# Twenty-four expert tiles' scores in plain float32, computed in the routing and table stages, in a transformer kernel with a product-key expert layer

## The chip, the cores and the metric

One Trainium2 chip, of which the kernel uses one core. The metric is the device time of one execution of the whole program in microseconds (us). Engines are named as in the profile: PE is TensorE (PEld its weight loads), DVE VectorE, ACT ScalarE, POOL GpSimd, SP SyncE, which here only issues DMAs.

## The reference, cut to what matters

A first block works on 512 tokens of width 1024 (a two-way gated recurrence, a convolution of 31 taps, attention, a merge, and an expert layer); a second block of two further layers follows. The change touches the convolution's place in time and the expert layer, which has 128 x 128 = 16384 experts:

```
def _peer(h, wq, k1, k2, u_tab, v_tab):
    def block(t):
        q = (t @ wq).reshape(PEER_BLOCK, PEER_HEADS, 2, PEER_DQ // 2)
        s1 = jnp.einsum('thd,nd->thn', q[:, :, 0], k1).astype(jnp.float32)
        s2 = jnp.einsum('thd,nd->thn', q[:, :, 1], k2).astype(jnp.float32)
        ...
        expert = (jnp.take_along_axis(i1, ci // PEER_TOPK, axis=-1) * PEER_NKEYS
                  + jnp.take_along_axis(i2, ci % PEER_TOPK, axis=-1))
        g = jax.nn.softmax(score, axis=-1).astype(t.dtype)
        act = jax.nn.gelu(jnp.einsum('thkd,td->thk', u_tab[expert], t))
        return jnp.einsum('thk,thkd->td', g * act, v_tab[expert]).astype(t.dtype)
```

## The kernel before, in words

The kernel is a row of phases with a barrier of all engines between them. Four of them matter here.

**Mixers** (`phase_mixers`). After eight recurrence heads come four rounds `attend(i)` of attention. In a round, DVE normalises and rotates the rows, and then goes through 8 units: the peak of the next unit's scores (L1476), a reciprocal (L1483), some convolution taps (`taps(count)`, L1435: one 128x512 multiply-add each, 248 in all, taken in order from a single list), and the rest part of a weight tile. ACT forms the softmax of a unit after its peak (L1206), normalises it (L1222), and copies out weight products; PE fills weight products between the transposes (L998). The hand-written order puts 8 taps ahead of the wait for `a_rstd` in rounds 1 to 3, 3 taps behind it, 10 taps in unit 0 and 7 in each other unit. When the list is used up, `taps` does nothing.

**Routing** (`phase_routing`). For each of 8 heads PE multiplies two query tiles (L1787, plain float32, 512 columns, 8 matmuls per half) and the key scores (L1795); ACT copies them out (L1818, L1823) and does the exponential of the head before (L1810); DVE finds the top 16 (from L1895 on), and POOL and DVE look up the indices.

**Table** (`phase_expert_table`). The choices of 384 of the 512 tokens are turned into a dense table of gate weights, 4 tokens a group, 96 groups. Per group DVE builds two one-hot tiles (L2000, L2004, rings of 4), PE multiplies them (L2016, four plain float32 matmuls of 128 columns), ACT copies the result out (L2027), and SP stores 4 MB to DRAM after each 16 groups (L2036).

**Experts** (`phase_experts`). The 384 tokens go through all 16384 experts densely: 128 tiles of 128 experts, 2 a step, 64 steps. Each tile has a score product (24 matmuls of 384 columns, L2205 to L2207: the operands are cut into an upper and a rest part of type float32r, and three of the four cross products are taken), a gelu (L2280), a multiplication with the table's rows (L2340), a cut of that product (L2285, L2325), and an output product into six PSUM banks (18 matmuls of 512 columns, L2221 to L2225). Both the tile of `peer_u` and that of `peer_v` (512 KB each) are cut by ACT (L2264, L2272) and DVE (L2325). PE's order in step s is: scores of step s+1, outputs of step s. The other 128 tokens' chosen rows are gathered by POOL with indirect DMAs (L2176, L2184), four of 512 KB a step, and handled by DVE (`dots`, L2351; `own_add`, L2367). DVE's order in step s: `cut_u(s+2)`, `cut_v(s+1)`, `dots(s+1)`, `weights(s)`, `weigh(s+1)`, two `own_add`. ACT's: `cut_u(s+2)`, `cut_v(s+1)`, `own_gelus(s)`, `gelus(s+1)`. ACT's `cut_v(s+1)` waits for the outputs of step s-1. Steps 0, 1, 62 and 63 are written out; the 60 between them are a loop with two steps in its body.

## Time and the profile before

| | us |
|---|---|
| median of 3 executions | 4812.54 (4811.25 to 4816.73) |
| the profiled execution | 4815.9 |
| its span in the profile | 4814.1 |
| attention rounds of the mixers | about 696 to 1085 |
| routing | about 1469 to 1677 |
| table | about 1678 to 1850 |
| experts | about 1850 to 2926 |

Over the span PE is busy 90%, DVE 55%, ACT 38%, POOL 11%. The profile is read by stage: a window of it gives each engine's busy time there, the granted clock of PE as a share of full speed, and the share of the 16 DMA engines' time that is used. Matmuls are pipelined, so that the time between two starts, not the duration of one, is what a matmul costs.

### The profile page before, as it was taken

How to read it: one execution, taken by the hardware profiler on the slowest of the kernel's cores; microseconds unless marked ns; L12 is line 12 of the kernel's file. 1: busy time of each engine (PE TensorE's matmuls, PEld its weight loads, DVE VectorE, ACT ScalarE, POOL GpSimd, SP SyncE). 2: the span in 40 equal slices, each digit the busy share in tenths (PEclk: the TensorE clock that was granted, in tenths of full speed). 3: DMA queues.
4: the chain of work that ended last, by engine and by line, in shares of the span. 5: the costliest groups of instructions: out<-in, count | busy, mean ns of one | idle time of the engine just before them, and what ended most of it. 6: DMA issues, size and time to landing. Idle time of an engine off the chain costs nothing. (4 is left out here: it accounts for less than half of the span.)

```text
span 4814.1 us, 56280 instructions
## 1 busy us (share of the span) xinstructions
PE 4348.4 (90%) x20979; PEld 3540.2 (74%) x20979; DVE 2663.7 (55%) x4645; ACT 1814.3 (38%) x2539; POOL 526.0 (11%) x308
## 2 busy tenths in 40 slices
PE   8988888879998367999999997999999999999998
PEld 6866765646874256999999995777878877777887
DVE  0777758773437897767677675334343333434332
ACT  1665654443421033333333333345232233643322
POOL 0000000000003502334333430000000000000000
PEclk9999999989999699999999998999999999999999
DMA  7111101103322037887787771211323322122332
GB/s 263 58 40 44 40 31 49 43 1 108 92 63 67 5 140 281 281 279 270 282 278 276 274 273 65 70 53 59 99 88 97 96 84 70 51 77 84 102 97 81
DMA packets 196090, 579.09 MB, mean 120 GB/s; under 512 B 17345, under 2 KB 66753, under 8 KB 194369
## 3 DMA queue, kind: packets, MB, share of 16 engines
q1 hardware_dynamic: 158032, 435.34, 27.4%
q0 software_dynamic: 36864, 134.23, 7.9%
q10 hardware_dynamic: 1008, 7.03, 0.4%
q8 instruction: 119, 1.95, 0.2%
q14 instruction: 67, 0.54, 0.0%
HBM read 549.27 MB, written 27.26 MB: 120 GB/s over the span
## 5 line engine op out<-in xcount | busy, mean ns | idle before, releaser
L402 DVE TENSOR_TENSOR tile_rest<-tile_raw,tile_up 128x1024 fp32r<-128x1024 f32 (+2 forms) x288 | 338.7, 1181 | 786.4 <-ACT tile_up L393 786.2
L410 PE MATMUL layer_psum<-hn_up,tile_up 128*128 128x512 f32 x1344 | 534.7, 398 | 21.5 <-DVE hn_rest L497 21.5
L411 PE MATMUL layer_psum<-hn_up,tile_rest 128*128 128x512 f32 x1344 | 527.7, 393 | 0.0
L412 PE MATMUL layer_psum<-hn_rest,tile_up 128*128 128x512 f32 x1344 | 527.3, 392 | 0.0
L393 ACT ACTIVATE tile_up<-tile_raw 128x1024 fp32r<-128x1024 f32 (+2 forms) x288 | 291.4, 1018 | 370.3 <-PE layer_psum L412 368.5
L2205 PE MATMUL ex_psum<-ex_t_up,ex_u_up 128*128 128x384 f32 x1024 | 344.5, 336 | 9.1 <-ACT ex_prod L2280 4.9
L2207 PE MATMUL ex_psum<-ex_t_rest,ex_u_up 128*128 128x384 f32 x1024 | 344.4, 336 | 0.0
L2206 PE MATMUL ex_psum<-ex_t_up,ex_u_rest 128*128 128x384 f32 x1024 | 343.9, 336 | 0.0
L410 PEld LDWEIGHTS layer_psum<-hn_up,tile_up 128*128 128x128 f32 x1344 | 255.7, 190 | 82.4 <-issue 30.0
L2225 PE MATMUL ex_psum<-ex_v_up,ex_prod_rest 128*128 128x512 f32 x768 | 300.0, 391 | 0.0
L2223 PE MATMUL ex_psum<-ex_v_rest,ex_prod_up 128*128 128x512 f32 x768 | 299.9, 390 | 0.0
L2221 PE MATMUL ex_psum<-ex_v_up,ex_prod_up 128*128 128x512 f32 x768 | 298.7, 389 | 0.0
L411 PEld LDWEIGHTS layer_psum<-hn_up,tile_rest 128*128 128x128 f32 x1344 | 255.6, 190 | 54.4 <-issue 1.9
L412 PEld LDWEIGHTS layer_psum<-hn_rest,tile_up 128*128 128x128 f32 x1344 | 255.1, 190 | 53.9
L2272 ACT ACTIVATE ex_v_up<-tT 128x1024 fp32r<-128x1024 f32 x128 | 128.8, 1052 | 290.3 <-PE ex_psum L2225 286.2
L2325 DVE TENSOR_TENSOR ex_v_rest<-tT,ex_v_up 128x1024 fp32r<-128x1024 f32 x128 | 151.2, 1222 | 143.9 <-ACT ex_v_up L2272 143.8
L601 PE MATMUL mx_psum<-x_up,mx_w_up 128*128 128x512 f32 x480 | 200.3, 417 | 9.4 <-DVE mx_w_rest L563 9.4
L2205 PEld LDWEIGHTS ex_psum<-ex_t_up,ex_u_up 128*128 128x128 f32 x1024 | 193.5, 189 | 12.5 <-issue 10.1
L1842 POOL TENSOR_TENSOR rt_hot<-rt_place,consts 128x1024 f32<-128x1024 f32 x16 | 30.8, 1928 | 1556.4 <-DVE rt_place L1952 1505.4
L2206 PEld LDWEIGHTS ex_psum<-ex_t_up,ex_u_rest 128*128 128x128 f32 x1024 | 193.4, 189 | 2.4
L2207 PEld LDWEIGHTS ex_psum<-ex_t_rest,ex_u_up 128*128 128x128 f32 x1024 | 193.2, 189 | 0.0
L602 PE MATMUL mx_psum<-x_up,mx_w_rest 128*128 128x512 f32 x480 | 190.9, 398 | 0.0
(450 smaller groups left out, 9981.3 us busy)
## 6 DMA issues: line engine op xcount, KB each, us to landing
ex_u<-in_peer_u SPq DMA_DIRECT2D x128, 512.0 KB, 4.3
tT<-in_peer_v SPq DMA_DIRECT2D x128, 512.0 KB
tile_raw<-in_w_gu SPq DMA_DIRECT2D x88, 512.0 KB, 3.6
xT<-in_w_head SPq DMA_DIRECT2D x56, 512.0 KB, 3.6
mod_w<-in_w_ada SPq DMA_DIRECT2D x48, 512.0 KB, 4.7
mg_w_raw<-in_w_merge SPq DMA_DIRECT2D x48, 512.0 KB
expert_table<-et_rows SPq DMA_DIRECT2D x6, 4096.0 KB
ex_rows<-expert_table SPq DMA_DIRECT2D x64, 384.0 KB, 6.2
```

The lines of the kernel that those rows point to most:

```text
L393: self.nc.scalar.activation(self.up[:, n % self.SLOTS, 0:blocks, :], self.raw[n % self.RAWS][:, 0:blocks, :], ACT.Copy).then_inc(self.up_r ...
L402: self.nc.vector.tensor_tensor(out=self.rest[:, n % self.SLOTS, 0:blocks, :], in0=self.raw[n % self.RAWS][:, 0:blocks, :], in1=self.up[:, ...
L410: self.nc.tensor.matmul(dst, w_up, up, start=first, stop=False)
L411: self.nc.tensor.matmul(dst, w_rest, up, start=False, stop=False)
L412: return self.nc.tensor.matmul(dst, w_up, rest, start=False, stop=last)
L601: self.nc.tensor.matmul(dst, w_up, up[:, d, :], start=d == 0, stop=False)
L2205: nc.tensor.matmul(dst, u_up[par, t][:, d, :], t_up[:, d, :], start=d == 0, stop=False)
L2206: nc.tensor.matmul(dst, u_rest[par, t][:, d, :], t_up[:, d, :], start=False, stop=False)
L2207: last = nc.tensor.matmul(dst, u_up[par, t][:, d, :], t_rest[:, d, :], start=False, stop=d == DB - 1)
L2221: nc.tensor.matmul(dst, prod_up[par, t][:, cols], v_up[par, t][:, rows, :], start=first, stop=False)
L2223: nc.tensor.matmul(dst, prod_up[par, t][:, cols], v_rest[par, t][:, rows, :], start=False, stop=False)
L2225: last = nc.tensor.matmul(dst, prod_rest[par, t][:, cols], v_up[par, t][:, rows, :], start=False, stop=final)
```

## The change

Three things are altered.

1. Of the 128 expert tiles, 24 (`EARLY`: tiles 2, 8, 13, 18, 24 and so on to 125, never two in a step) get their scores before the experts phase. A class `EarlyScores` loads such a tile of `peer_u`, multiplies it uncut with the tokens in plain float32 (8 matmuls of 384 columns in place of 24), applies gelu, and stores 128x384 numbers to DRAM. Twelve tiles are handled in routing (one each behind the key scores of heads 1 to 6, six behind those of head 7), and twelve in the table phase (one matmul ahead of each group's four).
2. In the experts phase those 24 tiles have no load or cut of `peer_u`, no score product and no gelu; their stored scores (192 KB) are loaded and DVE weighs them in place. The other 104 run through rings counted by their own number q. The loop over the steps is written out in full; so is SP's loop in routing.
3. The taps of the convolution are dealt anew: 14 in place of 8 ahead of the wait for `a_rstd` in rounds 1 to 3, 4 in place of 10 in unit 0 of all rounds.

```diff
+EARLY = [(2 * k + 1) * NKEYS // 48 for k in range(24)]
+EARLY_ROUTING = 12
...
                 if i > 0:
-                    taps(8)
+                    taps(14)
...
                         rests_behind(plan.chain[i][:2])
-                        taps(10)
+                        taps(4)
...
+class EarlyScores:
+    SLOTS = 3
+    def __init__(self, ph, io, mem, banks, first, count):
+        self.io, self.mem, self.banks, self.first, self.count = io, mem, banks, first, count
+        self.u = [ph.sb(f"early_u{n}", [P, DB, P]) for n in range(self.SLOTS)]
+        self.out = [ph.sb(f"early_out{n}", [P, T_DENSE]) for n in range(2)]
+        self.landed = [ph.sem(f"early_landed{n}") for n in range(self.SLOTS)]
+        self.stored = [ph.sem(f"early_stored{n}") for n in range(2)]
+        self.scored, self.gelu_ready = ph.sem("early_scored"), ph.sem("early_gelu_ready")
+    def load(self, sp, e):
+        if e >= self.count:
+            return
+        if e >= self.SLOTS:
+            sp.wait_ge(self.scored, START + e - self.SLOTS + 1)
+        sp.dma_start(self.u[e % self.SLOTS][:],
+                     self.io["peer_u"][EARLY[self.first + e]]).then_inc(self.landed[e % self.SLOTS], 16)
+    def store(self, sp, e):
+        sp.wait_ge(self.gelu_ready, START + e + 1)
+        sp.dma_start(self.mem.early[self.first + e], self.out[e % 2][:]).then_inc(self.stored[e % 2], 16)
+    def all_stored(self, sp):
+        for half in range(2):
+            sp.wait_ge(self.stored[half], START + 16 * len(range(half, self.count, 2)))
+    def block(self, nc, pe, e, d):
+        if d == 0:
+            pe.wait_ge(self.landed[e % self.SLOTS], START + 16 * (e // self.SLOTS) + 16)
+            if e >= 2:
+                pe.wait_ge(self.gelu_ready, START + e - 1)
+        ins = nc.tensor.matmul(self.banks[e % 2][:, 0:T_DENSE], self.u[e % self.SLOTS][:, d, :],
+                               self.mem.tT[:, d, 0:T_DENSE], start=d == 0, stop=d == DB - 1)
+        if d == DB - 1:
+            ins.then_inc(self.scored, 1)
+    def gelu(self, nc, act, e):
+        act.wait_ge(self.scored, START + e + 1)
+        if e >= 2:
+            act.wait_ge(self.stored[e % 2], START + 16 * (e // 2))
+        nc.scalar.activation(self.out[e % 2][:], self.banks[e % 2][:, 0:T_DENSE],
+                             ACT.Gelu_apprx_tanh).then_inc(self.gelu_ready, 1)
...
+        early = EarlyScores(ph, io, mem, (B[7], B[6]), 0, EARLY_ROUTING)
         block = ph.block(w)
+        def early_of(h):
+            return range(0) if h == 0 else range(h - 1, h if h < HEADS - 1 else EARLY_ROUTING)
         @block.sync
         def _(sp):
             sp.dma_start(keys[:], io["peer_k"]).then_inc(keys_loaded, 16)
-            with sp.Fori(0, HEADS // 2) as i:
-                for t in range(4):
+            for h in range(HEADS):
+                i, hh = h // 2, h % 2
+                for half in range(2):
+                    t = 2 * hh + half
                     load_tile(sp, w, 0, t, i, io["w_peer_q"][i * 2 + t // 2, t % 2])
+                if h == 1:
+                    for e in range(early.SLOTS):
+                        early.load(sp, e)
+                if h > 2:
+                    for e in early_of(h - 2):
+                        early.store(sp, e)
+                        early.load(sp, e + early.SLOTS)
+            for h in range(HEADS - 2, HEADS):
+                for e in early_of(h):
+                    early.store(sp, e)
+                    early.load(sp, e + early.SLOTS)
+            early.all_stored(sp)
...
+                for e in early_of(h):
+                    for d in range(DB):
+                        early.block(nc, pe, e, d)
...
+            pe.wait_ge(early.gelu_ready, START + EARLY_ROUTING)
...
+                for e in early_of(h):
+                    early.gelu(nc, act, e)
...
+        early = EarlyScores(ph, io, mem, (B[7], B[6]), EARLY_ROUTING, len(EARLY) - EARLY_ROUTING)
...
             for n in range(GROUPS):
+                early.block(nc, pe, n // DB, n % DB)
...
+                if n % DB == DB - 1:
+                    early.gelu(nc, act, n // DB)
         @block.sync
         def _(sp):
-            for turn in range(GROUPS // SUBS):
-                sp.wait_ge(unpacked, START + (turn + 1) * SUBS)
-                dst = mem.table[turn:turn + 1, :, :, :].rearrange("o p j t -> p (o j) t")
-                sp.dma_start(dst, rows[turn % 2][:]).then_inc(stored[turn % 2], 16)
+            for e in range(early.SLOTS):
+                early.load(sp, e)
+            for e in range(early.count):
+                if (e + 1) * DB % SUBS == 0:
+                    turn = (e + 1) * DB // SUBS - 1
+                    sp.wait_ge(unpacked, START + (turn + 1) * SUBS)
+                    dst = mem.table[turn:turn + 1, :, :, :].rearrange("o p j t -> p (o j) t")
+                    sp.dma_start(dst, rows[turn % 2][:]).then_inc(stored[turn % 2], 16)
+                early.store(sp, e)
+                early.load(sp, e + early.SLOTS)
+            early.all_stored(sp)
...
+        late = {j: q for q, j in enumerate(j for j in range(NKEYS) if j not in EARLY)}
+        soon = {j: k for k, j in enumerate(EARLY)}
+        def late_of(s):
+            return [late[j] for j in range(s * G, s * G + G) if j in late]
...
-        u_up, u_rest = ring("u_up", [P, DB, P], F32R), ring("u_rest", [P, DB, P], F32R)
+        u_up, u_rest = ([sb(f"{name}{n}", [P, DB, P], F32R) for n in range(4)] for name in ("u_up", "u_rest"))
+        early = [sb(f"early{n}", [P, N]) for n in range(2)]
...
+        def whole(j):
+            return early[soon[j] % 2][:] if j in soon else prod[:, j % G, :]
...
-            for s in range(2):
-                step(s, s % 2, s)
-            with eng.Fori(1, STEPS // 2 - 1) as i:
-                for par in range(2):
-                    step(i * 2 + par, par, None)
-            for s in range(STEPS - 2, STEPS):
+            for s in range(STEPS):
...
             def load_u(s, n):
-                for t in range(G):
-                    if begun(n, 1):
-                        sp.wait_ge(u_cut, START + (s - 1) * G + t + 1)
-                    sp.dma_start(u[t], io["peer_u"][s * G + t]).then_inc(u_landed[t], 16)
+                for j in range(s * G, s * G + G):
+                    if j in late:
+                        q = late[j]
+                        if q >= G:
+                            sp.wait_ge(u_cut, START + q - G + 1)
+                        sp.dma_start(u[q % G], io["peer_u"][j]).then_inc(u_landed[q % G], 16)
+                    else:
+                        k = soon[j]
+                        if k >= 2:
+                            sp.wait_ge(prod_cut, START + EARLY[k - 2] + 1)
...
             def scores(s, par, n):
-                for t in range(G):
-                    pe.wait_ge(u_cut, START + s * G + t + 1)
-                    if begun(n, 1):
-                        pe.wait_ge(gelu_ready, START + (s - 1) * G + t + 1)
-                    dst = B[t][:, 0:N]
+                for q in late_of(s):
+                    pe.wait_ge(u_cut, START + q + 1)
+                    if q >= 2:
+                        pe.wait_ge(gelu_ready, START + q - 1)
+                    dst = B[q % 2][:, 0:N]
+                    up, rest = u_up[q % 4], u_rest[q % 4]
                     for d in range(DB):
-                        nc.tensor.matmul(dst, u_up[par, t][:, d, :], t_up[:, d, :], start=d == 0, stop=False)
-                        nc.tensor.matmul(dst, u_rest[par, t][:, d, :], t_up[:, d, :], start=False, stop=False)
-                        last = nc.tensor.matmul(dst, u_up[par, t][:, d, :], t_rest[:, d, :], start=False,
-                                                stop=d == DB - 1)
+                        nc.tensor.matmul(dst, up[:, d, :], t_up[:, d, :], start=d == 0, stop=False)
+                        nc.tensor.matmul(dst, rest[:, d, :], t_up[:, d, :], start=False, stop=False)
+                        last = nc.tensor.matmul(dst, up[:, d, :], t_rest[:, d, :], start=False, stop=d == DB - 1)
                     last.then_inc(scored, 1)
...
             def cut_u(s, par, n):
-                for t in range(G):
-                    act.wait_ge(u_landed[t], START + s * 16 + 16)
-                    if begun(n):
-                        act.wait_ge(scored, START + (s - 1) * G)
-                    nc.scalar.activation(u_up[par, t][:], u[t], ACT.Copy).then_inc(u_up_ready, 1)
+                for q in late_of(s):
+                    act.wait_ge(u_landed[q % G], START + q // G * 16 + 16)
+                    if q >= 4:
+                        act.wait_ge(scored, START + q - 3)
+                    nc.scalar.activation(u_up[q % 4][:], u[q % G], ACT.Copy).then_inc(u_up_ready, 1)
...
             def gelus(s, par, n):
                 for t in range(G):
-                    act.wait_ge(scored, START + s * G + t + 1)
-                    if begun(n, 1):
-                        act.wait_ge(prod_cut, START + (s - 1) * G + t + 1)
-                    nc.scalar.activation(prod[:, t, :], B[t][:, 0:N], ACT.Gelu_apprx_tanh).then_inc(gelu_ready, 1)
-                    act.wait_ge(weighed, START + s * G + t + 1)
+                    j = s * G + t
+                    if j in late:
+                        q = late[j]
+                        act.wait_ge(scored, START + q + 1)
+                        if begun(n, 1):
+                            act.wait_ge(prod_cut, START + j - G + 1)
+                        nc.scalar.activation(whole(j), B[q % 2][:, 0:N], ACT.Gelu_apprx_tanh).then_inc(gelu_ready, 1)
+                    act.wait_ge(weighed, START + j + 1)
                     if begun(n):
                         act.wait_ge(step_filled, START + s - 1)
-                    nc.scalar.activation(prod_up[par, t][:], prod[:, t, :], ACT.Copy).then_inc(prod_up_ready, 1)
+                    nc.scalar.activation(prod_up[par, t][:], whole(j), ACT.Copy).then_inc(prod_up_ready, 1)
...
+                for q in late_of(s):
+                    cut(u_up_ready, u_cut, q + 1, u_up[q % 4][:], u[q % G], u_rest[q % 4][:])
...
             def weigh(s, par, n):
                 for t in range(G):
-                    dve.wait_ge(gelu_ready, START + s * G + t + 1)
+                    j = s * G + t
+                    if j in late:
+                        dve.wait_ge(gelu_ready, START + late[j] + 1)
+                    else:
+                        dve.wait_ge(early_landed[soon[j] % 2], START + soon[j] // 2 * 16 + 16)
                     dve.wait_ge(rows_landed[par], START + (s - par) * 8 + 16)
-                    part = prod[:, t, :].rearrange("p (b k) -> p b k", k=BLOCK)
+                    part = whole(j).rearrange("p (b k) -> p b k", k=BLOCK)
                     nc.vector.tensor_tensor(out=part, in0=part, in1=rows[par][:, :, t * BLOCK:(t + 1) * BLOCK],
                                             op=ALU.mult).then_inc(weighed, 1)
-                    cut(prod_up_ready, prod_cut, s * G + t + 1, prod_up[par, t][:], prod[:, t, :],
-                        prod_rest[par, t][:])
+                    cut(prod_up_ready, prod_cut, j + 1, prod_up[par, t][:], whole(j), prod_rest[par, t][:])
...
+            mem.early = nc.dram_tensor("early_scores", (len(EARLY), P, T_DENSE), F32, kind="Internal").ap()
```

## Rows read from the trace of the kernel before

**Rows 1.** windows: us, busy time by engine (count), PE clock, DMA share, GB/s

```profile
1875.00:1925.00 50.00, 49.00 (x239) 44.69 (x240) 39.19 (x51) 22.67 (x34) 20.23 (x13) 0.97 0.96 349
2100.00:2300.00 200.00, 200.00 (x1016) 182.42 (x1015) 140.90 (x182) 73.17 (x109) 78.44 (x49) 1.00 0.80 276
3500.00:4500.00 1000.00, 956.49 (x4379) 773.52 (x4378) 390.65 (x450) 367.23 (x434) 0.00 (x0) 0.98 0.27 82
```

**Rows 2.** timeline of PE in the experts: start us, duration us, line

```profile
2299.82 0.39 PE L2223 MATMUL ex_psum<-ex_v_rest,ex_prod_up 128*128 128x512 f32 x1
...
2303.45 0.39 PE L2225 MATMUL ex_psum<-ex_v_up,ex_prod_rest 128*128 128x512 f32 x1
2303.68 0.33 PE L2205 MATMUL ex_psum<-ex_t_up,ex_u_up 128*128 128x384 f32 x1
...
2309.94 0.33 PE L2205 MATMUL ex_psum<-ex_t_up,ex_u_up 128*128 128x384 f32 x1
...
2320.22 0.33 PE L2205 MATMUL ex_psum<-ex_t_up,ex_u_up 128*128 128x384 f32 x1
```

**Rows 3.** DVE in the same step; in brackets the idle time before

```profile
2305.03 2.36 DVE L2325 TENSOR_TENSOR ex_v_rest<-tT,ex_v_up 128x1024 fp32r<-128x1024 f32 x2 [2.27 <-ACT ex_v_up L2272]
2307.31 1.22 DVE L2351 CUSTOM_DVE_ANT_0 ex_more<-ex_more,ex_own_t 128x1024 f32<-128x1024 f32 x1
...
2314.37 2.60 DVE L2367 SCALAR_TENSOR_TENSOR ex_own_out<-tT,ex_weight,ex_own_out 128x1024 f32<-128x1024 f32 x2
2316.89 2.35 DVE L2325 TENSOR_TENSOR ex_u_rest<-ex_u,ex_u_up 128x1024 fp32r<-128x1024 f32 x2
```

**Rows 4.** DMA traffic of the experts, 2100 to 2900

```profile
DMA packets 92582, 218.96 MB, mean 274 GB/s; under 512 B 6879, under 2 KB 43743, under 8 KB 92580
...
q8 instruction: 1, 0.02, 0.0%
...
ex_u<-in_peer_u SPq DMA_DIRECT2D x94, 512.0 KB, 4.2
```

**Rows 5.** DMA traffic of the experts, 1875 to 1925

```profile
DMA packets 7503, 17.46 MB, mean 349 GB/s; under 512 B 561, under 2 KB 3633, under 8 KB 7499
```

**Rows 6.** DMA queues of a later stage, 3500 to 4500

```profile
q8 instruction: 35, 0.57, 0.2%
```

**Rows 7.** timeline of PE in routing

```profile
1503.10 13.90 PE L1787 MATMUL rt_psum<-tT,rt_w 128*128 128x512 f32 x32
1516.83 2.01 PE L1795 MATMUL rt_psum<-rt_keys,rt_qT 128*128 128x128 f32 x16
1518.68 13.90 PE L1787 MATMUL rt_psum<-tT,rt_w 128*128 128x512 f32 x32
```

**Rows 8.** timeline of ACT in routing, third head

```profile
1518.88 0.60 ACT L1823 ACTIVATE rt_s<-rt_psum 128x512 f32<-128x512 f32 x1 [0.36 <-PE rt_psum L1795]
```

**Rows 9.** timeline of DVE in routing, third head

```profile
1525.93 1.63 DVE L1895 MAX8 rt_val<-rt_s 128x8 f32<-128x128 f32 x8
```

**Rows 10.** timeline of PE at the end of routing

```profile
1673.91 2.15 PE L1802 MATMUL rt_psum<-consts,rt_found 128*128 128x128 f32 x9 [59.07 <-DVE rt_found L1885]
```

**Rows 11.** timeline of the table stage

```profile
1701.12 1.13 PE L2016 MATMUL et_psum<-et_second,et_first 128*128 128x128 f32 x8 [0.50 <-DVE et_second L2004]
...
1702.52 0.69 DVE L2000 TENSOR_TENSOR et_first<-consts,i1T 128x512 f32<-128x512 f32 x1
...
1702.75 1.13 PE L2016 MATMUL et_psum<-et_second,et_first 128*128 128x128 f32 x8 [0.50 <-DVE et_second L2004]
```

**Rows 12.** timeline of DVE in attention rounds 2 and 3

```profile
923.28 2.21 DVE L1454 SCALAR_TENSOR_TENSOR xT<-xT,params,at_work 128x1024 f32<-128x1024 f32 x2 [5.35 <-ACT at_work L1198]
...
943.50 7.83 DVE L1435 SCALAR_TENSOR_TENSOR convT<-at_upad,params,convT 128x512 f32<-128x512 f32 x10
...
1020.32 2.22 DVE L1454 SCALAR_TENSOR_TENSOR at_qk<-at_qk,params,at_work 128x1024 f32<-128x1024 f32 x2 [9.56 <-ACT at_work L1198]
```

**Rows 13.** timeline of PE in attention round 0, second unit

```profile
743.16 1.51 PE L998 MATMUL mx_psum<-consts,at_probs 128*128 128x128 f32 x6 [4.65 <-ACT at_probs L1222]
```

More of the change, by code:

```diff
@@ L1989, in phase_expert_table @@
         stored = [sem("stored0"), sem("stored1")]
+        early = EarlyScores(ph, io, mem, (B[7], B[6]), EARLY_ROUTING, len(EARLY) - EARLY_ROUTING)
+        assert early.count * DB == GROUPS
         block = ph.block()
@@ L2083, in phase_experts @@
         u_landed = [sem(f"u_landed{t}") for t in range(G)]
+        early_landed = [sem(f"early_landed{n}") for n in range(2)]
         v_landed = [sem(f"v_landed{t}") for t in range(G)]
@@ L2131, in load_u @@
             def load_u(s, n):
-                for t in range(G):
-                    if begun(n, 1):
-                        sp.wait_ge(u_cut, START + (s - 1) * G + t + 1)
-                    sp.dma_start(u[t], io["peer_u"][s * G + t]).then_inc(u_landed[t], 16)
+                for j in range(s * G, s * G + G):
[8 more added lines that the diff above has]
+                            sp.wait_ge(prod_cut, START + EARLY[k - 2] + 1)
+                        sp.dma_start(early[k % 2][:], mem.early[k]).then_inc(early_landed[k % 2], 16)
             def load_v(s, par, n):
@@ L2327, in cut_u @@
             def cut_u(s, par, n):
-                for t in range(G):
-                    cut(u_up_ready, u_cut, s * G + t + 1, u_up[par, t][:], u[t], u_rest[par, t][:])
+                for q in late_of(s):
+                    cut(u_up_ready, u_cut, q + 1, u_up[q % 4][:], u[q % G], u_rest[q % 4][:])
             def cut_v(s, par, n):
```

## The prediction

> **What bounds the kernel now.** I read the windows by stage first, then the timeline of PE inside a stage, then what DVE, ACT and the DMA queues do beside it. In the experts PE is the bound: in a window of 200 us it is busy for all 200, at full clock, while DVE is busy for 141, ACT for 73, and the DMA engines have a share of 0.80 [rows 1]. The reader is to see in the timeline that matmuls follow each other without a gap: 16 gaps between output matmuls take 3.63 us, 0.227 each, and 36 gaps between score matmuls 6.26 us, 0.174 each [rows 2]. A step is 2320.22 - 2303.68 = 16.54 us, which is 48 x 0.174 + 36 x 0.227 = 16.52. In the table stage it is DVE: it begins a group every 1.63 us and PE waits 0.50 us for it in each [rows 11]. In the last part of routing it is DVE with POOL: PE stands still for 59 us before the last transposes [rows 10]. In the attention rounds DVE, ACT and PE take turns, and PE waits 4.65 us in the second unit, behind DVE's ten taps [rows 12, 13].
>
> **Part 1, the score products taken out of the experts.** Each early tile removes 24 matmuls of 0.174 us, 4.18 us; 24 tiles make 100.2 us, all of it on the engine that sets the end. I take 100, if nothing else becomes the bound in the 24 shortened steps, which take 16.54 - 4.18 = 12.36 us.
>
> DVE: from its cut of v to the end of its cut of u it takes 2305.03 to 2319.24, 14.2 us with its waits [rows 3]. That is over 12.36, so in a shortened step DVE falls behind by up to 1.9 us, and gets back 2.3 in a full one; two shortened steps never follow each other, and a tile without a cut saves it half of 2.35 us once. What it falls behind with is the cut of v and the product of step s+1, which PE wants only after the scores of step s+2, some 12.4 + 8.3 us after the step's start. No wait of PE, cost 0. ACT is busy 37% and follows DVE.
>
> DMA: a step moves four loads and four gathers of 512 KB and 384 KB of rows, 4.59 MB, which at 16.54 us is 277 GB/s, as the traffic view has it (274) [rows 4]. A shortened step moves 4.26 MB (192 KB of stored scores in place of 512) in 12.36 us, 345 GB/s; the mean over the stage becomes (64 x 4.59 - 24 x 0.33) / 959 us = 298 GB/s. The highest rate shown is 349 GB/s, at a share of 0.96, in a stretch in which PE was busy 49 of 50 us [rows 1, 5]. Loads land in 4.2 us [rows 4] and are issued most of a step ahead. I take 0. The other end: if a shortened step moved only 274 GB/s it would take 15.5 us, 3.2 more, 76 us in all.
>
> The start of the stage loses a little: the second step's scores are shorter, and then PE waits for the first product. I take +1 (0 to +2).
>
> **Part 2, the loop written out.** PE is busy 200 of 200 us across some 12 step pairs and their branches, so there is nothing to win. The loop stays on the chip: one instruction packet in 800 us on queue q8 [rows 4]. Straight code fetches: 35 packets in 1000 us in a later stage [rows 6], in which PE issued 4379 matmuls and as many weight loads [rows 1], 250 instructions of PE a packet. The 64 steps hold 40 x 84 + 24 x 60 = 4800 matmuls and as many loads, some 39 packets, one per 25 us. The later stage takes them without PE stopping for long (956 us busy of 1000), though at a DMA share of 0.27; the 50 us of rows 5 hold written-out steps at 0.96. I take 0. The Trainium skill (Runtime: NRT & Kernel Launch, Instruction fetch mechanics) has the sequencer prefetch sequential code and warns of taken branches, not of straight code. By it the sum would be the same or better; the trace shows no cost of the branch.
>
> **Part 3, the same products in plain float32 in routing.** 16 matmuls of 512 columns take 1516.83 - 1503.10 = 13.73 us, 0.858 each [rows 7]; 384 columns are three quarters of that, 0.644, a tile 5.15 us. No row shows 384 columns, so the ends are 0.644 and 0.858. The third head's scores were copied out by 1519.5 [rows 8]; with one tile ahead of them it is 1524.6, and DVE takes them at 1525.93 [rows 9]: 1.3 us to spare. From there PE needs 15.6 (1518.68 - 1503.10) + 5.15 = 20.7 us a head, while DVE needs (1673.91 - 1525.93) / 6 = 24.7. PE's last six tiles end near 1523.8 + 5.15 + 4 x 20.7 + 15.6 + 30.9 = 1658, 16 us before the transposes that wait for DVE [rows 10]. SP, now with stores and loads between its weight tiles, waits for gelus that are done before the next tile's slot is free. ACT must change its function table twice a head, behind the copies that PE waits for. I take +1 (0 to +5, the third head at 0.858).
>
> **Part 4, the products in the table stage.** Per group PE has 8 records, half of 1518.68 - 1516.83 = 1.85 us, 0.925 [rows 7], plus 0.644, 1.57 us, against DVE's 1.63 [rows 11]. It fits by 0.06. The upper end, 0.858, gives 1.78 and 96 x 0.15 = +15 us. The stage also starts with a load of 4.2 us that PE must await, where it began 2 us behind DVE, and at a lower clock after that pause; DVE is held back by the ring of 4 once. I take +4 (0 to +15). The Trainium skill (FP8 and Floating Point Precision, TensorE Precision Notes) says true float32 takes 4 passes through the array: 4 x 0.174 = 0.70 as an estimate by that page, 1.62 us a group, still 0.01 under DVE; by it the sum stays and the margin is gone.
>
> At the end the store of the last scores stands behind a 4 MB store in SP's queue: +1 (0 to +2), with the phases' extra semaphores.
>
> **Part 5, the taps.** Ten taps take 7.83 us [rows 12], six 4.7. Taken out of unit 0 they let DVE give the next peak up to 4.7 us earlier, and PE's pause of 4.65 us there [rows 13] goes; all four rounds have one. Limits: the weight tile cut behind the taps must have been cut by ACT (half a us), so 4.2 a round, 17 in all (8 if units 1 to 7 are paced by PE's own work, 21 if the clock stays up too). The six taps set before `a_rstd` lie in idle time: 5.35 us in round 2 and 9.56 in round 3 [rows 12], against 4.7. If a round were without that idle, they would cost 4.7 there. The last round's extra taps fall where DVE waited for PE.
>
> **Sum** against the profiled execution (4815.9, span 4814.1): -100 + 1 + 0 + 1 + 4 + 1 - 17 = -110, so 4706. The median of the runs shown is 3.4 lower, so 4703.
>
> **Rivals.**
> *A, transfers set the shortened steps.* For it: 345 GB/s is close to the highest seen. Against: buffers reach over two steps, and the mean is only 298. At a rate halfway between 274 and 349, 312 GB/s, a shortened step takes 13.65 us, 1.3 more, 31 in all: 4734. It decides from where PE waits for a cut of u.
> *B, PE becomes the bound of the table stage.* 1.57 against 1.63 says little either way. With 0.1 us per group for the change between widths, 1.67 x 96 gives +4 beyond the stage's start, with 0.858 +11 beyond my +4: 4707 to 4714.
> *C, instruction fetch stops PE in the written-out experts (the other side).* 39 packets on engines that are 0.86 to 1 busy. If each were waited for as long as a load takes to land, 4.2 us, that is 164 us: 4867, slower. It turns to slower from 2.8 us a packet. Against it: straight steps ran at 49 of 50 us with the DMA engines at 0.96 [rows 1].
> *D, the taps bring nothing*, since PE paces the rounds anyway: 4720. Against it: PE's 4.65 us pause.
>
> **How the numbers follow.** My forecast 0.68, A 0.12, B 0.11, C 0.03, D 0.06. The forecast's own range is 4692 to 4715; A and D stretch the range to 4734, and the low end is taps at -21, table at 0 and the rest at their best. So 4690 to 4734, with about 0.15 left out. What this kernel's measurement can tell from no change is about 0.2%, 10 us; only C and a wide form of A come there or beyond: faster 0.96, same 0.01, slower 0.03.
>
> **What would show it.** In the profile after: score matmuls L2205's successors 832 each in place of 1024; PE busy near 100% in the experts and the stage some 99 us shorter; a shortened step of 12.4 us; the DMA share near 0.86; routing as long as before with PE busy to about 1658 on the old time axis; the table stage's idle time of PE per group fallen from 0.50 us to nearly none, and the distance of DVE's groups still 1.63; PE's pause of 4.65 us in the rounds gone. Wrong I would be if PE has idle time in the experts before a cut of u or by "issue", or if DVE waits for PE in each group of the table.

## The result and the profile after

The changed kernel takes 4688.7 us (median of 4 runs, 4684.14 to 4694.84) against 4814.64 (4 runs on the same chip, 4811.25 to 4816.99): ratio 0.974, 95% interval 0.9723 to 0.9757. It is 126 us faster. The forecast was 4703, with 4690 as the low end, so the time lies 1.3 us below the range.

The profiled execution took 4694.84 us, with a span of 4693.0, 121.1 less than before. Busy time over the whole span, and the instruction queue, from the profile page of the changed kernel:

```profile
PE 4343.6 (93%) x20787; PEld 3492.2 (74%) x20787; DVE 2632.9 (56%) x4621; ACT 1806.3 (38%) x2529; POOL 502.2 (11%) x308
q8 instruction: 156, 2.56, 0.2%
```

Windows of the changed kernel by stage (columns as in [rows 1]): the experts, the table stage, routing, the four attention rounds.

```profile
1875.00:2780.00 905.00, 905.00 (x4531) 817.72 (x4530) 677.02 (x889) 330.99 (x501) 371.13 (x242) 1.00 0.86 299
1655.00:1812.00 157.00, 155.03 (x960) 119.22 (x960) 154.78 (x475) 62.42 (x108) 0.00 (x0) 0.98 0.49 187
1445.00:1652.00 207.00, 190.64 (x584) 101.97 (x583) 163.77 (x938) 46.49 (x69) 112.45 (x48) 0.95 0.23 76
696.00:1070.00 374.00, 314.91 (x1288) 217.15 (x1288) 280.27 (x397) 173.73 (x223) 0.00 (x0) 0.94 0.10 31
```

The reader is to see in the first row that PE is busy for 905 of 905 us in the experts, with the DMA engines at a share of 0.86 and 299 GB/s, both as the prediction had them. The timeline of PE there shows a full step and a shortened one, each from the first output matmul to the next step's:

```profile
2064.22 0.39 PE L2315 MATMUL ex_psum<-ex_v_up,ex_prod_up 128*128 128x512 f32 x1
...
2080.77 0.39 PE L2315 MATMUL ex_psum<-ex_v_up,ex_prod_up 128*128 128x512 f32 x1
...
2093.16 0.39 PE L2315 MATMUL ex_psum<-ex_v_up,ex_prod_up 128*128 128x512 f32 x1
```

The distances of the starts are 16.55 us and 12.39 us; the prediction had worked out 16.54 and 12.36. Two more lines answer to [rows 10] and [rows 13], the last transposes of routing and the second unit of the first round (timeline of PE):

```profile
1648.88 2.15 PE L1871 MATMUL rt_psum<-consts,rt_found 128*128 128x128 f32 x9 [15.39 <-DVE rt_found L1956]
...
737.92 0.85 PE L1000 MATMUL mx_psum<-consts,at_probs 128*128 128x128 f32 x6 [0.52 <-ACT at_probs L1224]
```

PE's wait at the end of routing is 15.4 us in place of 59 (16 were predicted). Its pause in the unit is 0.5 in place of 4.65, and the same six matmuls take 0.85 us in place of 1.51.

Where the 121.1 us of the span lie, from the start times of the same instruction in both traces:

| stretch | before | after | difference | predicted |
|---|---|---|---|---|
| up to the first round | 696.3 | 695.2 | -1.1 | 0 |
| four attention rounds | 402.5 | 375.4 | -27.1 | -17 |
| merge (not touched) | 344.1 | 347.1 | +3.0 | 0 |
| the merge's last normalisation and routing, up to DVE's first group of the table | 235.2 | 235.6 | +0.4 | +1 |
| table, first to last group | 154.6 | 155.5 | +0.9 | +4 |
| last group to PE's first matmul of the experts | 17.3 | 17.8 | +0.5 | +1 |
| experts, up to the last output matmul | 1073.8 | 973.1 | -100.7 | -99 |
| the rest (not touched) | 1890.3 | 1893.3 | +3.0 | 0 |

The two untouched stretches differ as much between traces of kernels that are alike there (the merge 344.1 to 347.1 us, the rest 1884 to 1893). The row that stands apart is the rounds.

The table stage of the changed kernel, to lay beside [rows 11], PE and then DVE (timeline):

```profile
1701.20 1.05 PE L2090 MATMUL et_psum<-et_second,et_first 128*128 128x128 f32 x8
1702.09 0.81 PE L1771 MATMUL et_psum<-tT,et_early_u 128*128 128x384 f32 x2
1702.74 1.05 PE L2090 MATMUL et_psum<-et_second,et_first 128*128 128x128 f32 x8
```

```profile
1699.74 0.68 DVE L2073 TENSOR_TENSOR et_first<-consts,i1T 128x512 f32<-128x512 f32 x1
...
1701.37 0.68 DVE L2073 TENSOR_TENSOR et_first<-consts,i1T 128x512 f32<-128x512 f32 x1
...
1703.00 0.68 DVE L2073 TENSOR_TENSOR et_first<-consts,i1T 128x512 f32<-128x512 f32 x1
```

DVE still begins a group every 1.63 us; the idle 0.50 us of PE has become the 0.65 us of the 384-column products.

### The profile page after: what moved, and what is told of

It is laid out like the page before. It is cut to its first block and busy times, and to the rows that moved or that the text cites. A ratio compares the mean times of both kernels' runs of the same rounds, so it can differ in the third digit from the quotient of the medians.

```text
span 4693.0 us, 54122 instructions
## 1 busy us (share of the span) xinstructions
PE 4343.6 (93%) x20787; PEld 3492.2 (74%) x20787; DVE 2632.9 (56%) x4621; ACT 1806.3 (38%) x2529; POOL 502.2 (11%) x308
## 5 line engine op out<-in xcount | busy, mean ns | idle before, releaser
L2300 PE MATMUL ex_psum<-ex_t_up,ex_u_up 128*128 128x384 f32 x832 | 279.9, 336 | 4.3 <-DVE ex_u_rest L2421 4.3
L2302 PE MATMUL ex_psum<-ex_t_rest,ex_u_up 128*128 128x384 f32 x832 | 279.8, 336 | 0.0
L2301 PE MATMUL ex_psum<-ex_t_up,ex_u_rest 128*128 128x384 f32 x832 | 279.5, 336 | 0.0
L605 PE MATMUL mx_psum<-x_rest,mx_w_up 128*128 128x512 f32 x480 | 189.8, 395 | 0.0
L1437 DVE SCALAR_TENSOR_TENSOR convT<-at_upad,params,convT 128x512 f32<-128x512 f32 x240 | 179.9, 750 | 7.3
L159 DVE TENSOR_TENSOR mg_w_rest<-mg_w_raw,mg_w_up 128x1024 fp32r<-128x1024 f32 x56 | 68.5, 1225 | 198.9 <-ACT mg_w_up L153 198.9
```

The costliest lines, as they stand in the source:

```text
L2300: nc.tensor.matmul(dst, up[:, d, :], t_up[:, d, :], start=d == 0, stop=False)
L2301: nc.tensor.matmul(dst, rest[:, d, :], t_up[:, d, :], start=False, stop=False)
L2302: last = nc.tensor.matmul(dst, up[:, d, :], t_rest[:, d, :], start=False, stop=d == DB - 1)
```

## The experiments

**Which half of the change gives what: e1_taps and e2_early.** The first is the kernel before with the new deal of the taps alone, the second is the changed kernel with the old deal:

```
-                    taps(8)
+                    taps(14)
...
-                        taps(10)
+                        taps(4)
```

> The kernel before with the taps alone dealt anew (14 and 4). Theory one, order and clock: the shorter unit 0 takes 24 x 0.78 = 19 us off DVE's path at most, and PE, which no longer pauses for 4.65 us, keeps its full clock through rounds 0 and 1, which gives another 8 us: 26 to 28 us less than before, about 4788, with the rounds' granted clock at 0.93 to 0.94 in place of 0.90. Theory two, order alone, as the prediction had it: 17 us less, 4798. Theory three, the gain of the rounds comes with the rest of the change: under 10 us less.

> The changed kernel with the taps as before (8 and 10). If the two halves of the change add up and the taps give 27 us, this is 99 us under before, about 4716. The prediction's terms for this part were -100 + 1 + 1 + 4 + 1 = -93, 4722. If the stages interact it is off the sum with the run of the taps alone by more than 5 us.

Measured: e1_taps 4788.54 us, ratio 0.995 (0.9936 to 0.9964), against 4812.36 for the kernel before on that chip: 24 us faster. e2_early 4711.94, ratio 0.9788 (0.9774 to 0.9801): 100 us faster. Together that is 124 of the 126. So the taps gave 24, where 17 was the sum's term and 21 its end; the early tiles gave 100, where -93 was in the sum. Of the theories for e1_taps the second (17 us, order alone) fell short; the first asked for 26 to 28 and got 24, with the granted clock of 0.93 that it named.

The same 1288 matmuls of the four rounds, in windows of e2_early (old deal), e1_taps and e3_half (below):

```profile
696.00:1097.00 401.00, 327.60 (x1288) 226.30 (x1288) 279.54 (x396) 173.43 (x224) 0.00 (x0) 0.90 0.09 29
```

```profile
696.50:1075.20 378.70, 316.79 (x1288) 217.47 (x1288) 281.01 (x397) 175.02 (x224) 0.00 (x0) 0.93 0.10 31
```

```profile
697.00:1082.60 385.60, 318.91 (x1288) 220.32 (x1288) 281.05 (x398) 175.09 (x224) 0.00 (x0) 0.93 0.10 31
```

With the new deal PE is busy 10.8 us less for the same work, at a granted clock of 0.93 in place of 0.90. The rounds are 23.7 us shorter, so the other 12.9 are waits that went. Only the waits had been in the sum. How long PE runs at the lower of its two levels (1.2 GHz, against 2.4) can be told from a mean: 0.90 over 401 us is some 2 x 0.10 x 401 = 80 us. The trace's record of the clock has 78.6 us in the rounds before, 51.3 in e1_taps and 47.8 in the changed kernel. (The 74.5 and 44.0 in two of the expectations below are some 4 us too low: 74.5 of 402.5 us would be a mean of 0.91, and the window shows 0.90.)

Round 1 shows it best. Its window in the kernel before, and in e1_taps:

```profile
800.12:910.38 110.26, 96.04 (x454) 72.36 (x454) 76.86 (x108) 47.90 (x63) 0.00 (x0) 0.95 0.13 42
```

```profile
795.72:897.26 101.54, 91.66 (x454) 69.07 (x454) 76.93 (x108) 47.91 (x64) 0.00 (x0) 1.00 0.14 46
```

8.7 us shorter, 4.4 of them busy time of the same 454 matmuls. In the timeline of PE in the kernel before, the round starts at the lower clock, and after the pause of 4.68 us it falls to it once more:

```profile
801.86 4.97 PE L969 MATMUL mx_psum<-at_work,consts 128*128 128x512 f32 x8 [2.27 <-ACT at_work L1191]
...
843.94 1.51 PE L998 MATMUL mx_psum<-consts,at_probs 128*128 128x128 f32 x6 [4.68 <-ACT at_probs L1222]
```

and in e1_taps neither happens:

```profile
797.46 3.27 PE L969 MATMUL mx_psum<-at_work,consts 128*128 128x512 f32 x8 [2.27 <-ACT at_work L1191]
...
833.82 0.85 PE L998 MATMUL mx_psum<-consts,at_probs 128*128 128x128 f32 x6 [0.64 <-ACT at_probs L1222]
```

**Half of the taps: e3_half**, from the kernel before:

```
-                    taps(8)
+                    taps(11)
...
-                        taps(10)
+                        taps(7)
```

> The kernel before with half the shift: 11 taps ahead of the wait and 7 in unit 0. If only DVE's order matters, it gives half of what 14 and 4 give: 9 us if they give 17, 13 if they give 27. If the clock has a part that depends on the length of PE's pause, a pause of 2.3 us in place of 4.65 keeps the clock up as well and gives more than half: 16 us or more of 27, with the lower clock after the second unit of rounds 0 and 1 gone.

Measured: 4794.65 us, ratio 0.9961 (0.9947 to 0.9975), 18 us faster. Half of the move brings three quarters of the gain. In its timeline of PE half of the pause of round 1 is left:

```profile
838.26 0.85 PE L998 MATMUL mx_psum<-consts,at_probs 128*128 128x128 f32 x6 [2.28 <-ACT at_probs L1222]
```

and yet the round is 103.2 us against 110.3 before and 101.5 in e1_taps, with the clock at full level throughout and the matmuls at 0.85. The gain does not go with the pause's length alone. The expectation had the lower clock gone from round 0 too, and there it stayed: behind a pause of the same 2.28 us PE fell to the lower level for 3.4 us (6.8 before).

```profile
741.58 1.51 PE L998 MATMUL mx_psum<-consts,at_probs 128*128 128x128 f32 x6 [2.28 <-ACT at_probs L1222]
```

**More ahead, none taken from unit 0: e4_start**, from the kernel before:

```
-                    taps(8)
+                    taps(14)
```

> The kernel before with 14 taps ahead of the wait and still 10 in unit 0. Unit 0 is as long as before in all rounds, so PE's pause of 4.65 us and the lower clock behind it stay. Eighteen taps move out of the last round's units into idle time. If the gain comes from unit 0: under 6 us, from the last round alone. If it comes from filling the idle time ahead of the wait: 14 us.

Measured: 4829.25 us, ratio 1.0031 (1.002 to 1.0042), 17 us slower. That missed: no theory on record had a cost here. The timeline of DVE in round 3 of e4_start shows it:

```profile
1006.20 7.84 DVE L1435 SCALAR_TENSOR_TENSOR convT<-at_upad,params,convT 128x512 f32<-128x512 f32 x10
1035.77 0.69 DVE L1428 TENSOR_TENSOR at_upad<-at_conv_a,at_conv_g 128x512 f32<-128x512 f32 x1 [21.73 <-ACT at_conv_g L1035]
...
1044.83 2.21 DVE L1454 SCALAR_TENSOR_TENSOR at_qk<-at_qk,params,at_work 128x1024 f32<-128x1024 f32 x2
```

The taps are one list in order, and each eighth part of it starts with an operand that PE must have multiplied and ACT copied out. Six more taps a round, taken nowhere else, bring DVE to the head of such a part before it is there: it stands for 21.73 us behind it, with the work behind `a_rstd` queued after the taps. It begins 28.7 us after the round's start (1044.83 - 1016.09), in the kernel before 11.4 (1020.32 [rows 12] - 1008.88). Round 1 has the same kind of wait, 5.6 us against 1.0 before. Rounds 1 and 3 become 6.3 and 11.4 us longer, 17.7 together, which is the whole loss. So the four taps left in unit 0 do two things: they let the peak go first, and they keep the list from running ahead of its operands. The prediction had only the first.

**The clock alone: e5_fill.** PE gets work in its pause, DVE's order is unchanged (`FILL` has 5, 5, 5 and 8 matmuls for the second unit of the rounds, nobody reads their result):

```
+                    for _ in range(FILL.get((i, u), 0)):
+                        nc.tensor.matmul(B[0], mem.c("ident"), mem.c("cos2"), start=True, stop=True)
                     pe.wait_ge(prob_ready, START + i * UNITS + u + 1)
```

> The kernel before (ten taps in unit 0), with plain float32 matmuls of 512 columns into an unused bank, whose result nobody reads, put where PE stands still for DVE's peak in the second unit of each round: 5, 5, 5 and 8 of them, 4.3 us (6.9 in the last round) at full clock. DVE's order is not changed. Theory 1 (the new deal of the taps gains by the clock as well as by the pause): the half-clock time in the four rounds, 74.5 us before and 44.0 after the change, falls to some 50 to 60 us, each us of it is worth up to 0.5, so 4 to 9 us faster, in rounds 1 and 3 above all, while the unit's own start stays where it was. Theory 2 (only the order of DVE counts, the lower clock in the trace lies in time that PE would have waited anyway): no change, or up to 3 us slower for what the matmuls push back.

Measured: 4810.28 us, ratio 0.9992 (0.9983 to 1.0001): by the ratio 4 us, not told from nothing by the times alone. The traces say more: half-clock time in the rounds 58.1 us against 78.6, the rounds 399.0 against 402.5. In round 1, from the first unit's transposes to those of a later unit (31.56 to 76.15 us after the round's start before, 31.57 to 73.40 in e5_fill) 2.8 us went, although PE still gets its probabilities no earlier; that is what the new deal takes off the same units beyond the pause (2.7). In rounds 0, 2 and 3 the other 14 us of full clock brought only 0.8: there PE catches up with the next wait. Theory 1 holds in kind, its 4 to 9 us at most at the low end (4 by the ratio, 3.5 in the trace). In e1_taps, where the waits went too, 27.3 us less at the lower level came with 10.8 us less busy time, 0.40 each; here 20.5 us less shortened the rounds by 3.5, 0.17 each. The Trainium skill (TensorE: Matmul & The Clock Gate, Terms) prices throttled time at about itself times one minus the clock's share, here a half. By it the 6.8 us that went from round 1 are an estimated 3.4 us; the trace shows 2.8 there, and much less in the rounds where PE had waits.

**The straight code alone: e6_straight**, the kernel before with all 64 steps written out:

```
-            for s in range(2):
+            for s in range(STEPS):
                 step(s, s % 2, s)
-            with eng.Fori(1, STEPS // 2 - 1) as i:
-                for par in range(2):
-                    step(i * 2 + par, par, None)
-            for s in range(STEPS - 2, STEPS):
-                step(s, s % 2, s)
```

> The kernel before with the experts' loop written out over all 64 steps, and nothing else changed. My theory: 0, within 3 us; PE stays at 100% busy, some 40 instruction packets more on its queue, a step still 16.5 us. Rival (fetching straight code stops PE): 40 packets times up to 4.2 us, up to +160; already one tenth of that, 16 us, would show. Second rival (the branches of the loop cost PE): 29 branches fewer, 3 us and more faster.

Measured: 4813.98 us, ratio 0.9995 (0.9986 to 1.0004). The experts' window, and the instruction queue in 2100 to 2900, where the loop had 1 packet [rows 4]:

```profile
2100.00:2300.00 200.00, 200.00 (x1016) 182.50 (x1015) 140.84 (x182) 72.79 (x109) 78.99 (x49) 1.00 0.79 277
```

```profile
q8 instruction: 33, 0.54, 0.3%
```

33 packets, and PE never stops. Neither the fetching nor the loop's branches show a cost: the interval is 0.14% down and 0.04% up, and PE was at 200 of 200 us with either. The Trainium skill (Runtime: NRT & Kernel Launch, Instruction fetch mechanics) says that sequential code is prefetched; the trace agrees.

**The margin of the table stage: e8_margin** (the changed kernel with one more matmul of 128 columns in each group, nobody reads its result).

```
                 last.then_inc(packed, 1)
+                nc.tensor.matmul(B[5][:, 0:P], mem.c("ident"), mem.c("ident"), start=True, stop=True)
```

> The changed kernel with one more plain float32 matmul of 128 columns per group of the table stage, whose result nobody reads: 96 of 0.23 us. My theory (PE needed 1.57 us a group against DVE's 1.63, a margin of 0.06): PE needs 1.80, the stage becomes longer by 0.17 x 96 = 16 us against the changed kernel, about 4705, and DVE waits for PE in every group. Rival 1 (the margin was nil, PE already paced the stage): 22 us, about 4711. Rival 2 (PE still has slack that the records hide): under 5 us.

Measured: 4708.58 us, ratio 0.9777 (0.9764 to 0.9791), against 0.974: by the ratios 18 us more than the changed kernel. Two groups in its timeline of PE:

```profile
1700.16 1.06 PE L2090 MATMUL et_psum<-et_second,et_first 128*128 128x128 f32 x8
1701.06 0.39 PE L2093 MATMUL et_psum<-consts 128*128 128x128 f32 x2
1701.28 0.81 PE L1771 MATMUL et_psum<-tT,et_early_u 128*128 128x384 f32 x2
1701.93 1.05 PE L2090 MATMUL et_psum<-et_second,et_first 128*128 128x128 f32 x8
```

PE needs 1.77 us a group without a gap: 0.90 for the four products, 0.22 for the added matmul, 0.65 for the 384 columns. DVE's groups are 1.76 apart. Without the added one PE needs 1.55 and DVE's own 1.63 sets the stage, a margin of 0.08. The stage grew by 12.2 us from first to last group and its end by 4.0, 16 as expected. Rival 1 (no margin) asked for 22, rival 2 for under 5. The 18 us of the times lie between 16 and 22; what speaks against rival 1 is the distance of the groups, 1.63 without the added matmul where PE needs 1.55. Little is named as a wait in this trace (0.9 us of DVE for PE in all); it is read from the distances between starts.

**What is left of the clock: e9_after_fill**, the changed kernel with the loop of e5_fill (`FILL` has all eight units of round 3 and two of round 2, 21 matmuls together, not the 26 of the expectation) and this, which nobody reads either:

```
+                for _ in range((0, 2, 3, 2)[i]):
+                    nc.tensor.matmul(B[1], mem.c("ident"), mem.c("cos2"), start=True, stop=True)
                 pe.wait_ge(a_squared, START + i + 1)
```

> The changed kernel with plain float32 matmuls of 512 columns, whose result nobody reads, in the waits that PE has left in the attention rounds: 0, 2, 3 and 2 at the start of rounds 0 to 3, and 26 spread over rounds 2 and 3, mostly ahead of the transposes of each unit. Half-clock time in the rounds is 44.0 us now, 33.8 of it in rounds 2 and 3. Theory 1 (the clock in the rounds is worth something by itself): half of that goes, some 17 us, worth up to 8: 3 to 8 us faster than the changed kernel. Theory 2 (PE's matmuls are not what the last round waits for, or the added ones stand in the way): 0 to 5 us slower.

Measured: 4686.49 us, ratio 0.9732 (0.9718 to 0.9745), 2 us less than the changed kernel by the medians, within the intervals. In the trace the rounds are 373.0 us against 375.4 with 23.9 us at the lower level against 47.8: 2.4 us for 23.9, below Theory 1's 3 to 8. (Rounds 2 and 3 of the changed kernel have 40.9 us at the lower level by the record, not 33.8.) The last round is hardly set by PE: in e10_best (below), with the same fillers, its window has PE at a granted clock of 0.92, in the changed kernel at 0.81, and is 1.2 us shorter.

```profile
985.90:1067.70 81.80, 66.91 (x203) 35.78 (x201) 51.63 (x78) 33.36 (x44) 0.00 (x0) 0.92 0.00 0
```

```profile
987.60:1070.60 83.00, 55.48 (x166) 31.42 (x166) 51.72 (x78) 33.36 (x44) 0.00 (x0) 0.81 0.00 1
```

**More tiles: e7_more and e10_best.** e7_more is the changed kernel with 27 early tiles, e10_best has the fillers of e9 besides.

```
-EARLY = [(2 * k + 1) * NKEYS // 48 for k in range(24)]
-EARLY_ROUTING = 12
+EARLY = [(2 * k + 1) * NKEYS // 54 for k in range(27)]
+EARLY_ROUTING = 15
```

> The changed kernel with 27 early tiles in place of 24, the three more in routing behind the key scores of the last head (15 there, 12 in the table stage as now). My theory (an early tile takes 4.18 us off the experts as long as routing hides its 5.15): the experts become 12.5 us shorter; PE has about 16 us between its last early tile and the transposes that wait for DVE, and three tiles take 15.5 of them, so routing stays as long: 4676, 12 to 13 us faster than the changed kernel. Rival 1 (that room is smaller, the tiles push the transposes back): up to 15 us given back, nothing gained. Rival 2 (more shortened steps make the transfers the bound): PE has idle time in the experts, less than 8 us gained.

> The kernel with 27 early tiles and, besides, the matmuls into an unused bank in the waits of the attention rounds, as tried in the changed kernel, where the rounds became 2.4 us shorter in the trace and the median 2 us lower. If the two add up: 14 to 16 us faster than the changed kernel, 4673 to 4676. If the gain from the matmuls was chance: the same as with 27 tiles alone.

Measured: e7_more 4677.6 us, ratio 0.9719 (0.9705 to 0.9732), 11 us less than the changed kernel; e10_best 4671.7, ratio 0.971 (0.9697 to 0.9723), 17 us less. Experts from PE's first matmul to the last output 960.4 us against 973.1: 12.7 for three tiles (12.5 expected). The transposes of routing in e7_more, timeline of PE:

```profile
1650.59 1.18 PE L1871 MATMUL rt_psum<-consts,rt_found 128*128 128x128 f32 x9 [2.92 <-DVE rt_found L1956]
```

and a window of its experts:

```profile
1875.00:2750.00 875.00, 875.00 (x4370) 789.26 (x4369) 660.10 (x868) 321.83 (x486) 361.56 (x240) 1.00 0.88 304
```

PE has no idle time in the experts at 304 GB/s, so rival 2 does not hold. Rival 1 holds in part. The wait of 15.39 us became 2.92, 12.5 less, where three tiles take 15.5: the transposes start 3.0 us later than in the changed kernel, counted from the last head's key scores (51.4 us behind them against 48.4). The timelines of ACT and DVE show what they now wait for:

```profile
1647.70 0.49 ACT L1780 ACTIVATE rt_early_out<-rt_psum 128x384 f32<-128x384 f32 x1 [4.67 <-PE rt_psum L1771]
1648.21 1.28 ACT L1879 ACT_TABLE_LOAD   x1
1649.51 0.26 ACT L1879 ACTIVATE rt_ex<-rt_ex 128x64 f32<-128x64 f32 x1
```

```profile
1649.80 0.22 DVE L1954 TENSOR_REDUCE rt_z<-rt_ex 128x4 f32<-128x64 f32 x1 [2.92 <-ACT rt_ex L1879]
```

The last head's exponential stands behind the gelus of all early tiles in ACT's order, with a table load of 1.28 us ahead of it; in the changed kernel it starts at 1635.32, before DVE needs it, and here DVE waits 2.92 us for it. The nine transposes run at full clock (1.18 us against 2.15), so that the stretch up to the table is 1.8 us longer in all (237.4 against 235.6). The 2.92 us that PE still waits are no room: a fourth tile would push the exponential, and with it the transposes, back by an estimated 5.15 us, the time of a tile (not tried). e10_best is the fastest kernel of this study; its intervals overlap those of e7_more, and the rounds in its trace are shorter by 2.5 us, as in e9.

## Why the prediction was wrong, step by step

*The step that failed is the term for the taps (part 5).* The prediction put 17 us as the limit of the pauses, and 21 "if the clock stays up too". e1_taps measured 24, the trace of the changed kernel 27. It is a term that was mis-sized: the pause that was to go went, and what went with it was put too low. It passed its own end of 21 by 3 us, more than the 1.3 us by which the time lies below the range. Two errors lie in it. The pauses did go (4.65 to 0.5), but the waits of PE over the four rounds fell by only 13 us, since some come back before other units (1.24 us in round 0). And the clock stood at nothing in the sum and at 4 us in its end, where the busy time of the same matmuls fell by 10.8: 27 us fewer at 1.2 GHz, each costing up to half a us. How much of the 10.8 would have come by the clock alone is not shown; e5_fill got 3.5 us with DVE's order unchanged. The row for it was at hand: the 1.51 us of [rows 13] against 0.85 at full clock is a matmul group right behind the pause at the lower level, and a window of the kernel before gives a granted clock of 0.90 over 400 us. That clock should have been priced by the stretch.

*Part 1, the experts:* right. 100.7 us less in the trace, 24 x 4.18 = 100.3; shortened step 12.39 us. Rival A (transfers) refuted, PE had no idle time at 299 GB/s here nor at 304 in e7_more. Loads landed later (median 5.2 us against 4.2), at no cost.

*Part 2, the loop written out:* right, 0; e6_straight. Rival C with its 164 us refuted.

*Part 3, routing:* right to within 1 us (+0.4). The 16 us between PE's last early tile and the transposes were 15.4; as room for tiles they were 12.5, since ACT's last exponential stands behind the gelus (e7_more). The prediction's check of ACT in routing had only the copies that PE waits for.

*Part 4, the table:* 1.57 against 1.63 was right (1.55, a margin of 0.08), the +4 for its start was not: PE does wait 5.7 us for the first load, but the stage is just 0.9 us longer, since DVE went on into its ring and was held up for 0.7 us. Rival B refuted by e8_margin, which needed 0.22 us a group more to reach it. The end of the table and the start of the experts: +0.5 for +1, and nothing for the start of the experts, which is within the 3.0 us by which that stage differs between the traces of the changed kernel and of e8_margin. These small terms held 7 us; about 2 came.

*Rival D* (the taps bring nothing) refuted by e1_taps.

By the medians the taps brought 7 us more than their term and the early tiles 7 us more than theirs (100 for 93), of which the small terms are the largest part: half of the distance to the forecast is theirs. In the span: taps -10 beyond the sum, experts -2, small terms -4, the untouched stretches +5: -11. The profiled execution of the changed kernel was also its slowest of four, 6 us above the median, which the forecast could not know. With the taps at 24 the forecast would have been 4696.

## What to carry to other kernels

Where PE's granted clock is below 1 in a stage that an edit relieves of pauses, price the clock as a term of its own: half-clock time that goes away times at most a half. Here it came with 0.40 of busy time where the waits went too (e1_taps), and brought 0.17 where they stayed (e5_fill) and 0.10 where little was left to gain (e9_after_fill). Before moving items forward in an ordered list, look for the operand at its head: six taps more a round, with none taken out behind, turned a gain of 24 us into a loss of 17. Work put under a stage that another engine sets is free up to the room read from the timeline, on every engine that the work touches: PE had 15.4 us (16 read), and of the 15.5 us of three more tiles 12.5 were free and 3.0 came back through ACT's order.

## What the runs showed that was not expected

In one run, e3_half, PE was at full level through the whole of round 1 with half of the pause left (2.28 us), and fell to the lower level behind the same pause of 2.28 us in round 0. The pause's length alone does not settle it. And the same code in the rounds (new deal, no fillers) gave 375.4, 375.4, 378.8 and 379.1 us in four traces (the changed kernel, e7_more, e1_taps, e8_margin), with 47.8, 47.9, 51.3 and 54.7 us at the lower level. With the old deal three traces (the kernel before, e2_early, e6_straight) agree: 402.5 us, 78.6 of them at the lower level, each time. How the clock falls in a stage with pauses can thus go with some 4 us of a single profile with no edit behind it.
